# Layer 1's input projection in seven block products per step, and the retention of all heads between the output projection's tiles

## The reference

```
proj = rms_norm(y) @ w_in_ret                       # 2048 x 12288
q, k (256 a head, rotated), v (512 a head), g (512 a head)
per head and chunk of 128 tokens:
  scores = (q @ k^T) * decay
  o      = scores @ v + (q @ s_prev) * exp(log_g * (i + 1))
  s_new  = exp(log_g * 128) * s_prev + (k * dec)^T @ v
out = (head_rms_norm(o) * silu(g)) @ w_out_ret      # 4096 x 2048
y   = y + rms_norm(out)
```

## Time and profile before

| | |
|---|---|
| runs | 3608.27, 3610.52, 3620.78 us |
| profiled execution, span | 3613.4 us |
| TensorE busy | 3486.5 us, 96%, 26244 matmuls |
| VectorE busy | 1666.8 us, 46% |
| ScalarE busy | 980.5 us, 27% |
| HBM read, written | 566.09 MB, 70.65 MB |

### The profile page before, as it was taken

One profiled execution on the slowest core, in us unless ns is written; L12 is line 12 of the kernel. 1 busy time (PEld: TensorE's weight loads), 2 busy tenths in 40 slices (PEclk: granted clock), 3 DMA queues, 4 the chain that ended last, 5 costly groups with the idle time before them and its releaser, 6 DMA issues.

```text
span 3613.4 us, 65176 instructions
## 1 busy us (share of the span) xinstructions
PE 3486.5 (96%) x26244; PEld 3103.5 (86%) x26244; DVE 1666.8 (46%) x2689; ACT 980.5 (27%) x1552; POOL 68.1 (2%) x87
## 2 busy tenths in 40 slices
PE   7999999999999999888999999999999999999998
PEld 7987887788788877588999898989899999989998
...
GB/s 175 154 203 214 269 281 258 261 286 265 262 266 282 279 256 278 223 144 142 132 83 168 82 170 82 172 85 164 88 156 93 153 99 144 157 128 105 108 123 123
DMA packets 472175, 642.60 MB, mean 178 GB/s; under 512 B 35649, under 2 KB 294850, under 8 KB 468738
## 3 DMA queue, kind: packets, MB, share of 16 engines
...
HBM read 566.09 MB, written 70.65 MB: 176 GB/s over the span
## 4 chain that ended last, share of the span: by engine, by line
PE 87%; DVE 4%; DMA 3%; issue 2%; ACT 2%; SPq 1%; ACTq 0%; POOL 0%; DVEq 0%; POOLq 0%
PE low_banks L1004 68%; PE high_banks L1004 16%; PE high_banks L1007 3%; DMA area<-in_cache_v 2%; DVE WL L1565 1%; SPq L949 1%; DVE area L1661 1%; ACT WH L1285 1%; DMA WR<-in_w_in_attn 0%; ACT area L1348 0%; DVE area L1634 0%; ACT XH L1285 0%; DVE area L1946 0%; DMA area<-in_cache_k 0%; DVE XL L1570 0%
## 5 line engine op out<-in xcount | busy, mean ns | idle before, releaser
L1004 PE MATMUL low_banks<-XH,WH 128*128 128x288 f32 (+2 forms) x6656 | 1524.8, 307 | 43.7 <-DVE XL L1570 18.4
L1004 PE MATMUL low_banks<-XH,WL 128*128 128x288 f32 (+2 forms) x6656 | 1457.1, 297 | 0.0
L1004 PE MATMUL low_banks<-XL,WH 128*128 128x288 f32 (+2 forms) x6656 | 1455.2, 296 | 0.0
L1004 PEld LDWEIGHTS low_banks<-XH,WH 128*128 128x128 f32 x6656 | 1082.7, 190 | 194.2 <-issue 148.9
L1004 PEld LDWEIGHTS low_banks<-XL,WH 128*128 128x128 f32 x6656 | 1087.1, 190 | 0.0
L1004 PEld LDWEIGHTS low_banks<-XH,WL 128*128 128x128 f32 x6656 | 1085.7, 190 | 0.0
L1565 DVE TENSOR_TENSOR WL<-WR,WH 128x1024 fp32r<-128x1024 f32 x436 | 528.7, 1213 | 753.8 <-ACT WH L1285 749.2
L1285 ACT ACTIVATE WH<-WR 128x1024 fp32r<-128x1024 f32 x436 | 461.4, 1058 | 1144.4 <-PE low_banks L1004 897.9
L1004 PE MATMUL high_banks<-area 128*32 128x256 f32 (+9 forms) x4720 | 630.4, 466 | 35.1 <-DMA area<-in_cache_v 16.8
L1004 PEld LDWEIGHTS high_banks<-area 128*32 128x32 f32 (+3 forms) x4720 | 271.6, 138 | 249.6 <-issue 177.5
L1661 DVE STREAM_TRANSPOSE area<-area 128x512 f32<-128x512 f32 x512 | 335.5, 691 | 121.2 <-PE high_banks L1004 63.2
...
## 6 DMA issues: line engine op xcount, KB each, us to landing
area<-in_cache_k SPq DMA_DIRECT2D x512, 256.0 KB, 5.0
area<-in_cache_v SPq DMA_DIRECT2D x512, 256.0 KB, 5.5
WR<-in_w_in_ret SPq DMA_DIRECT2D x200, 512.0 KB, 3.6
...
```

What stands on the lines that cost most here:

```text
L1004: return nc.tensor.matmul(out, a, b, start=start, stop=stop, skip_group_check=True)
```

## The change

Of the 48 input steps of layer 1 the first three and the last three stay as they are. The other 42 are done in seven block products each (Strassen's algorithm in Winograd's form): the 2048 x 256 weights are cut into four quarters a11 to a22, the 576 tokens into two halves of 288 and the rows into two halves of 1024. Sums of quarters (`quad_sum`, s1 to s4) and of token blocks (`x_rec`, `x_mix`, t1 to t4) are multiplied, 8 slices x 3 matmuls of 128x288 each, and the results are put together in PSUM and SBUF by `product_drain`. The split weights stand in a ring of three. All inputs of the retention, the six direct steps' too, are written to HBM (`mixed_d`) and read again by head (`load_qk`, `load_v4`, `load_g4`).

The token mixes stand in `norm_between`, which now spans 160 tiles instead of 64. The retention of all eight heads then runs in the last stage, 64 tiles a head: 96 tiles of the last three input steps, then the output projection, which now works in eight parts of 512 rows, so with twice as many additions on VectorE.

```
+PRODUCTS = ("a11", "s2", "s1", "s3", "a12", "s4", "a22")
+X_OF = (0, "t2", "t1", "t3", 1, 2, "t4")
+BANK_OF = (0, 1, 2, 1, 0, 2, 1)
+FILL = 96
+PER_HEAD = 64
...
+    def split(self, m):
+        if m >= self.count:
+            return []
+        n, i = divmod(m, 7)
+        self.splits[m] = Stage("quad_split", r=n % 2, what=PRODUCTS[i], slot=(m + 2) % 3, summed=self.sums.get((n, PRODUCTS[i])))
+        out = [self.splits[m]]
+        if i == 0:
+            out += self.sum(n, "s2")
+        if i == 4:
+            out += self.sum(n, "s4")
+        if i == 5:
+            out += self.sum(n + 1, "s1")
+        if i == 6:
+            out += self.sum(n + 1, "s3") + self.load()
+        return out
...
+    def product(self, m):
+        n, i = divmod(m, 7)
+        freed = {0: (n - 2, 4), 1: (n - 2, 6), 2: (n - 2, 5), 3: (n, 1), 4: (n, 0), 5: (n, 3), 6: (n, 3)}[i]
+        self.mm[m] = Stage("product", i=i, bank=3 * (n % 2) + BANK_OF[i], slot=(m + 2) % 3, ready=self.splits[m],
+                           freed=self.drains.get(freed), mixed=self.mixes.get(X_OF[i]), opening=m == 0)
+        out = [self.mm[m]]
+        if i != 2:
+            self.drains[n, i] = Stage("product_drain", i=i, o=n % 2, bank=3 * (n % 2) + BANK_OF[i], other=3 * (n % 2) + 2)
+            out.append(self.drains[n, i])
+        if i == 0 and n:
+            out += self.store(n - 1)
+        return out
...
+def retention_work(h, stored):
 
     at = {}
 
     def put(t, *s):
-        at.setdefault(t, []).extend(s)
+        at.setdefault(max(t, -PER_HEAD * h), []).extend(s)
+    loads = retention_loads(h, stored)
+    early = 0 if h else 13
+    if h:
+        put(-40, loads["v"])
+        put(-20, loads["q"], loads["k"])
+        put(-14, Stage("load_head"))
+        for k in range(8):
+            put(6 + 2 * k + (2 if k > 3 else 0), Stage("load_state", b=2 * (k % 4) + k // 4))
+    for which in range(2):
+        for part in range(3):
+            put(-12 + early + 5 * which + 2 * part, Stage("rope", which=which, part=part))
     for hh in range(2):
         for j in range(3):
-            put(32 * (3 + hh) + 2 + 2 * j, Stage("natural", what="r", hh=hh, j=j))
-    for which in range(2):
-        for part, t in enumerate((1, 4, 7)):
-            put(32 * (which + 1) + t, Stage("rope", which=which, part=part))
-    put(100, Stage("load_head"))
-    for b in range(NB):
-        put(110 + 4 * b, Stage("load_state", b=b))
-    put(129, Stage("rs_keys"))
-    put(138, Stage("pad_rows"))
-    put(152, Stage("rs_mask"))
+            put(5 * hh + 2 * j, Stage("natural", what="r", hh=hh, j=j))
+    put(7, loads["g"])
+    put(20, Stage("silu_g"))
+    put(12, Stage("rs_keys"))
+    put(13, Stage("pad_rows"))
+    put(21, Stage("rs_mask"))
     for c in range(4):
-        put(139 + 12 * c, Stage("ret_scores", c=c))
-        put(144 + 12 * c, Stage("ret_out", c=c))
-        put(146 + 12 * c, Stage("ret_state", c=c))
-    put(187, Stage("store_state_p"))
-    put(190, Stage("ret_rstd", t=0, n=4))
+        put(14 + 9 * c, Stage("ret_scores", c=c))
+        put(17 + 9 * c, Stage("ret_out", c=c))
+        put(18 + 9 * c, Stage("ret_state", c=c))
+    put(48, Stage("store_state_p"))
+    put(47, Stage("ret_rstd", t=0, n=4))
+    put(49, Stage("rs_out"))
+    put(54, Stage("ret_rstd", t=4, n=1))
     for t in range(4):
-        put(195 + 2 * t, Stage("ret_norm", t=t))
-        put(200 + 6 * t, Stage("gate", t=t))
-        put(202 + 6 * t, Stage("store_ret", t=t))
-    put(228, Stage("rs_out"))
-    put(236, Stage("ret_rstd", t=4, n=1))
-    put(242, Stage("ret_norm", t=4))
-    put(248, Stage("gate", t=4))
-    put(250, Stage("store_ret", t=4))
+        put(50 + t, Stage("ret_norm", t=t))
+        put(52 + 3 * t, Stage("gate", t=t))
+        put(54 + 3 * t, Stage("store_ret", t=t))
+    put(57, Stage("ret_norm", t=4))
+    put(64, Stage("gate", t=4))
+    put(66, Stage("store_ret", t=4))
     for g in range(2):
         for e in range(2):
-            put(254 + 6 * (2 * g + e), Stage("rs_state", g_=g, e=e))
+            put(56 + 3 * (2 * g + e), Stage("rs_state", g_=g, e=e))
         for j in range(4):
-            put(262 + 16 * g + 4 * j, Stage("store_state", b=2 * j + g))
+            put(61 + 7 * g + 2 * j, Stage("store_state", b=2 * j + g))
+    if h < HEADS:
+        kt = CH * (h % 2)
+        put(72, Stage("load_x", part=h % 2, kt=kt, row=CH * h, width=T, layer=1))
+        for k in range(CH):
+            put(78 + 2 * k, Stage("split_x", part=h % 2, kt=kt + k, width=T))
...
+    rec = lambda q, buf, by: [Stage("x_rec", q=q, buf=buf, by=by)]
+    mix = lambda to: [Stage("x_mix", to=to)]
     at = {3: lambda: n.transpose(2), 4: lambda: n.square(3), 8: lambda: n.scale(3), 12: lambda: n.square(4), 20: lambda: n.transpose(3),
-          24: lambda: n.scale(4), 36: lambda: n.transpose(4)}
-    for t in range(2 * 32):
+          24: lambda: n.scale(4), 25: lambda: rec((0, 0), 2, "pool"), 26: lambda: rec((1, 0), 4, "pool"),
+          36: lambda: n.transpose(4), 40: lambda: rec((1, 1), 3, "dve"), 46: lambda: rec((0, 1), 1, "dve"), 52: lambda: mix(3),
+          54: lambda: prods.load() + prods.load(), 58: lambda: mix(1),
+          64: lambda: mix(2), 70: lambda: mix(4)}
+    for k, to in enumerate((2, 1, 3, 4)):
+        prods.mixes[f"t{to}"] = Stage("x_mix_split", to=to)
+    at.update({t: (lambda to=to: [prods.mixes[f"t{to}"]]) for t, to in ((76, 2), (86, 1), (96, 3), (106, 4))})
+    at.update({112: lambda: prods.sum(0, "s1"), 116: lambda: prods.sum(0, "s3"), 150: lambda: prods.split(0), 153: lambda: prods.split(1)})
+    for t in range(5 * 32):
...
+            proj.step("out1", s * 256, [CH * part], [CH * (part % 2) + k for k in range(CH)], span=span, kind="+" if part else "y", hh=s, layer=1)
...
+            def product(g, i, bank_, slot, ready, freed, mixed, opening):
+                pe.wait_ge(sem["w_lo"], c.after(ready, "w_lo"))
+                if opening:
+                    for n in ("proj0_drained", "proj1_drained", "x_lo", "drained4", "drained5"):
+                        pe.wait_ge(sem[n], c.before(n))
+                if freed is not None:
+                    for n in adds(freed):
+                        pe.wait_ge(sem[n], c.after(freed, n))
+                if mixed is not None:
+                    pe.wait_ge(sem["mix_lo"], c.after(mixed, "mix_lo"))
+                (wh, wl), (xh, xl) = ring(slot), tokens(X_OF[i])
+                for k in range(8):
+                    for n, (a, x) in enumerate(((wh, xh), (wh, xl), (wl, xh))):
+                        last = mm(bank[bank_][:, 0:HALF], a[:, k, :], x[:, k, :], start=i < 3 and k == 0 and n == 0, stop=k == 7 and n == 2)
+                last.then_inc(sem["w_used"], 1)
...
+            def quad_sum(g, r, what):
+                dve.wait_ge(sem[f"quads_in{r}"], c.before(f"quads_in{r}"))
+                dve.wait_ge(sem["w_lo"], c.before("w_lo"))
+                a11, a12, a21, a22 = [quad(r, n) for n in ("a11", "a12", "a21", "a22")]
+                to, a, b, op = {"s1": (first_sum, a21, a22, ADD), "s3": (a21, a11, a21, SUB), "s2": (a11, first_sum, a11, SUB),
+                                "s4": (a11, a12, a11, SUB)}[what]
+                v.tensor_tensor(to, a, b, op).then_inc(sem["quad_sums"], 1)
+                dve.wait_ge(sem["quad_sums"], c.done("quad_sums"))
...
+            def product_drain(g, i, o_, bank_, other):
+                if i in (0, 4):
+                    return
+                dve.wait_ge(sem["w_used"], c.before("w_used"))
+                dve.wait_ge(sem["half_act"], c.before("half_act"))
+                here, first = bank[bank_][:, 0:HALF], staged[:, 2 * o_ + 1, 0:HALF]
+                c12, c22 = staged[:, 2 * o_, HALF:T], staged[:, 2 * o_ + 1, HALF:T]
+                if i == 1:
+                    last = v.tensor_tensor(c12, here, first, ADD)
+                if i == 3:
+                    o.link(v.tensor_tensor(c22, here, first, ADD))
+                    last = v.tensor_tensor(c22, bank[other][:, 0:HALF], c22, ADD)
+                if i == 5:
+                    last = v.tensor_tensor(c12, here, c12, ADD)
+                if i == 6:
+                    last = v.tensor_tensor(first, here, first, ADD)
+                last.then_inc(sem["half_dve"], 1)
+                dve.wait_ge(sem["half_dve"], c.done("half_dve"))
```

420 lines of the change are left out of this document (308 added, 112 removed).

## The result

The kernel after takes **3733.2 us** (median of 4 runs, 3729.2 to 3741.0), the kernel before 3609.4 (4 runs on the same chip, 3606.9 to 3620.8): 1.0346 times as long, 95% interval 1.0325 to 1.0367. I had forecast 3641, slower by 0.8%, within 3565 to 3695. The direction was right, the size was not: 92 us are missing, and the time lies outside the range. The profiled execution took 3740.97 us, its span is 3739.0, against 3644 predicted: 95 to explain.

The account below looks back on a forecast made before the run. TensorE, busy 96% of the span, was taken as the bound. Terms -134.4 - 12.5 + 12 + 104 + 22.6 + 31 + 8 = +31 on 3613.4 gave a span of 3644, carried to the median as 3641 us; range 3565 to 3695.

Parts of the forecast that it names:

- The products, -134.4: Layer 1's input steps: 1008 fewer matmuls at 0.1333 us each, with the product stage at TensorE's pace, save 134.4 us.
- Rival 4: Product stage not at TensorE's pace: 294 products each 0.2 us late, +59; chance 0.15 together with rival 3.
- The token splits, -12.5: Output projection: earlier waits and clock falls at splits of the gated retention vanish, splits standing 12 to 18 tiles ahead; -12.5 us.
- A wait at a head's start, +22.6: Before a head's first output: padding copies hold ScalarE's queue; 3.0 us for 7 heads, 1.6 for head 0, +22.6.
- The dense stretch, +104: Tiles 49 to 66 of a head: VectorE bounds, TensorE waits 15 us per head for heads 2 to 6; +104 overall.
- Rival 1 (half absorbed): Dense stretch: VectorE's lateness half absorbed, costing 52, its clock falls 15; total -37, 3573 us; chance 0.24.
- The mixes, +12: Stage between the layers: VectorE's token mixes and weight splits cost 10 us of waiting and one clock fall; +12, 0 to 25.
- The clock, +31: Last stage: TensorE runs at half clock after idle gaps, in the dense stretch and after head-start waits; +31, 0 to 60.
- 5: End of the kernel: the last eight output steps have half the tiles to cover the last sums; +5 us.
- Rival 2 (clock stays up): Last stage: stalls as walked but the clock stays up, 3610 us, no change; chance 0.15.
- Heads 105 to 110 us apart: Last stage: sign of a right forecast, stores of the gated retention 105 to 110 us apart per head instead of 187.
- rival 3: Lateness spreads: another 1 to 2 us per chunk over 32 chunks, +50, 3690 us; chance 0.15 together with rival 4.

Follow-up runs that it names:

- experiment 1: Kernel after, with the four token splits of a head's output rows eight tiles later: 3671.0 us, ratio 1.0174 to the kernel before.
- experiment 12: Kernel after, with token splits eight tiles later and counted by semaphores of their own: 3641.4 us, ratio 1.0078 to the kernel before.
- experiment 4: Kernel after, with the first eight block loads of the product stage spread over tiles 55 to 148: 3732.5 us, ratio 1.0345.
- experiment 6: Kernel after, with GpSimd's two 128x2304 sums given to VectorE: 3733.4 us, ratio 1.0344 to the kernel before.
- experiment 10: Kernel of experiment 9, with the first head's six transposes of v three tiles later: 3600.0 us, ratio 0.9969 to the kernel before.
- experiment 9: Kernel after, with token splits, state loads and stores, and rotation later, block loads spread, GpSimd's sums on VectorE, rs_out earlier, last norm later: 3600.6 us.

## Why the prediction was right in direction and wrong in size

- **The products, -134.4.** Right, and a little more. One product of 24 matmuls lasts from 1901.82 to 1904.99, 3.17 us, 0.1320 a matmul against 0.1333 in the earlier trace rows; TensorE is 100% busy. That accounts for the stage of 294 products, 931 us where I had 941. Rival 4 is out.
- **The token splits, -12.5: the step that failed.** I booked them as free because they "stand 12 to 18 tiles ahead of their use". TensorE waited 79.0 us for them, and the clock fell behind the eight waits of 10 us. How far ahead of its use a step stands says nothing of the step's own inputs: its load stood six tiles ahead of it, and those tiles lasted nine of the 14.8 us that it took. I laid out every queue's instructions in the dense stretch, and no transfers at all. Experiments 1 and 12 show the cost: with the splits later and counted apart, the kernel takes 3641.4 us. That this is the forecast to the microsecond is chance, since other terms were off both ways. That the place and the counting of these splits cost 92 us in this kernel is shown; 69 of the 90 us in the last stage are waits and 21 the clock.
- **A wait at a head's start, +22.6.** Right place, wrong cause. The mechanism I gave (ScalarE held by eight padding transfers, 5.1 us) is in the trace, and is worth some 6 us in experiments 1 and 12, not 22.6: without the token split, ScalarE has room to catch up before the mask.
- **The dense stretch, +104.** Right in kind, a fifth too large. The three rows of waits sum to 83.4 (45.0 + 22.1 + 16.3). One head, wait by wait, in the timeline of after, TensorE; I had 1.8, 2.1, 1.0, 3.1, 1.0, 1.2 and, before the second natural, 2.0, with three smaller ones between:

```profile
3124.68 0.66 PE L1230 MATMUL high_banks<-eye_sb,area 128*128 128x128 f32 x4 [1.58 <-DVE area L2199]
3129.58 0.91 PE L1230 MATMUL high_banks<-eye_sb,area 128*128 128x128 f32 x4 [1.84 <-DVE area L2199]
...
3138.36 0.66 PE L1230 MATMUL high_banks<-eye_sb,area 128*128 128x128 f32 x4 [2.91 <-DVE area L2199]
3140.75 2.09 PE L1227 MATMUL high_banks<-area 32*128 32x512 f32 x8 [0.94 <-DVE area L2220]
3148.76 1.14 PE L1227 MATMUL high_banks<-area 32*128 32x512 f32 x8 [1.03 <-DVE area L2220]
...
3158.71 0.63 PE L1230 MATMUL high_banks<-eye_sb,area 128*128 128x128 f32 x4 [1.97 <-DVE area L2207]
```

  Six of the waits I walked are there, within 0.3 us and in the same order (1.8, 2.1, 3.1, 1.0, 1.2 and 2.0); the 1.0 ahead of the first state update is not. Rival 1 (half absorbed) is out: 83 of 104 came.
- **The mixes, +12.** Measured +26. The price of a 128x2304 operation, 2.56 us, was exact. TensorE waited 23.1 us there for weight splits (before, 6.4, and 1.6 for another operation of VectorE), where I had booked 10 more. What I left out: GpSimd's two sums, which I had counted as taken off VectorE, slow VectorE's weight splits fivefold while they run, and the weights behind the eight block loads come late (5.7 us). Experiments 4 and 6 took these two away one at a time and the time did not move, so what each is worth is not shown. The rest goes with a granted clock of 0.79 in the mixes' window. The sum lies just above the end of my range of 0 to 25.
- **The clock, +31.** Too small. In the last stage +94 is what must be explained. TensorE's idle time there is 205 us (1035.8 less 830.7), where I had booked 132 (104, 22.6 and 5): +73, of which the token wait in place of the 22.6 is +56, the dense stretch -21, and the waits that I had not in the sum the rest. The clock can be read by itself: the same matmuls keep TensorE busy for 830.7 us in the kernel after and for 800.3 in experiment 10, at a mean granted clock of 0.92 and 0.97. Added up from the clock records of the traces, TensorE was busy at the 1.2 GHz level for 114 us of this stage in the kernel after and for 47 in experiment 10; over the 13 kernels profiled, from the kernel after to experiment 12, the busy time grows by 0.44 us with each such us. My estimate from that slope is 0.44 x 114, some 50 us, where I had 31: +20. The two make the 94 to within 1 or 2 us. Rival 2 (clock stays up) is out: the clock fell.
- **Heads 105 to 110 us apart.** The stores of the first gate of heads 0 and 7 are at 2784.3 and 3590.5, 115.2 apart on average; in experiment 9 it is 98.8 (2765.9 to 3457.5).
- **Range.** It held the terms' own bounds, and none for a resource that I had not looked at. In time rival 4 (+59, so 3700) and rival 3 (3690) came closest, neither by what happened: no product was late. Rival 3 did name the token splits in front of the score masks, but priced them by their own duration, spread over 32 chunks, and not by one wait for a load per head.
